# A residual turned round: tokens on the partitions, wide weights moving, gates as rows

## The reference

```python
h = rms_norm(x, gain) * (1 + scale) + shift      # shift, scale, gate come from a condition vector
y = stage(h)                                      # attention mixer, swiglu, conv/ssm mixer
x = x + gate * rms_norm(y, gain2)                 # first block (4 steps: f0, cd, f1, f2 follow them)
x = x + f * gate * y                              # second block (3 steps: in2, f3, end follow them)

def rms_norm(x, w):                               # over the 1024 features of a token
    return x * rsqrt(mean(x * x, axis=-1) + 1e-6) * w

def swiglu(h, w_in, w_out):                       # 1024 -> 2 x 2816 -> 1024, four times
    gate, up = split(h @ w_in, 2)
    return (silu(gate) * up) @ w_out
```

## Time and profile before

| what | value |
|---|---|
| median of three runs | 1353.5 us (1351.81 to 1355.49) |
| the profiled execution | 1355.59 us, its span 1353.7 us |
| TensorE, busy | 1240.0 us, 92% of the span |
| VectorE, busy | 956.0 us, 71% |
| ScalarE, busy | 598.1 us, 44% |
| GpSimd, busy | 84.1 us, 6% |
| chain that ended last | PE 79%, DVE 13%, ACT 4%, DMA 3% |

### The profile page before, as it was taken

The page is one execution under the profiler, slowest core; times in us unless marked ns, Lnnn a source line. Parts: engine busy times, 40 slices in busy tenths (PEclk is TensorE's granted clock), DMA queues, the critical chain, the costliest instruction groups (busy, mean ns, idle before and its releaser), DMA issues.

```text
span 1353.7 us, 22880 instructions
## 1 busy us (share of the span) xinstructions
PE 1240.0 (92%) x9892; PEld 1169.3 (86%) x9892; DVE 956.0 (71%) x1555; ACT 598.1 (44%) x977; POOL 84.1 (6%) x117
## 2 busy tenths in 40 slices
PE   2797979899999897889999999999999888999997
PEld 1686648899999796779999989999999887999996
DVE  5974565888885875468887768887755946655554
ACT  1533354443444445454444445444443254544442
POOL 0000000000000100019600010000000000000000
PEclk9897689999999998999999999999999998999999
DMA  9880304378895391127786644777741323455540
GB/s 379 318 330 24 164 1 187 127 305 315 315 335 210 137 397 53 63 78 266 276 303 261 265 170 169 306 298 294 275 184 64 125 93 125 145 209 212 216 153 31
DMA packets 39300, 276.78 MB, mean 204 GB/s; under 512 B 4368, under 2 KB 4896, under 8 KB 6304
## 3 DMA queue, kind: packets, MB, share of 16 engines
q1 hardware_dynamic: 37152, 269.27, 52.7%
q0 software_dynamic: 1040, 3.70, 0.8%
q10 hardware_dynamic: 1008, 2.37, 0.5%
HBM read 273.72 MB, written 1.07 MB: 203 GB/s over the span
## 4 chain that ended last, share of the span: by engine, by line
PE 79%; DVE 13%; ACT 4%; DMA 3%; issue 1%; POOL 0%; SPq 0%; DVEq 0%; ACTq 0%
PE PS L377 77%; DVE LO L1274 2%; DMA raw<-WS 2%; DVE raw L1264 2%; PE PS L561 1%; DMA SC<-scratch 1%; ACT RS L895 1%; DVE TMP L1308 1%; DVE HLo L1303 1%; ACT HH L895 1%; DVE TMP L1334 1%; ACT HI L895 1%; DVE X L1338 1%; ACT SC L895 1%; DVE RS L1289 0%
## 5 line engine op out<-in xcount | busy, mean ns | idle before, releaser
L377 PE MATMUL PS<-HH,HI 128*128 128x256 f32 x1940 | 557.1, 287 | 39.5 <-ACT HH L895 23.5
L377 PE MATMUL PS<-HLo,HI 128*128 128x256 f32 x1940 | 559.2, 288 | 1.4 <-DVE HLo L1316 0.4
L377 PE MATMUL PS<-HH,LO 128*128 128x256 f32 x1940 | 553.3, 285 | 0.0
L1274 DVE TENSOR_TENSOR LO<-raw,HI 128x1024 fp32r<-128x1024 f32 x340 | 403.7, 1226 | 123.0 <-ACT HI L895 123.0
L377 PEld LDWEIGHTS PS<-HH,HI 128*128 128x128 f32 x1940 | 376.8, 194 | 45.4 <-ACT HH L895 27.0
L895 ACT ACTIVATE HI<-raw 128x1024 fp32r<-128x1024 f32 x340 | 339.5, 1049 | 119.1 <-PE PS L377 86.6
L377 PEld LDWEIGHTS PS<-HLo,HI 128*128 128x128 f32 x1940 | 376.0, 194 | 6.6 <-DVE HLo L1303 4.0
L377 PEld LDWEIGHTS PS<-HH,LO 128*128 128x128 f32 x1940 | 377.0, 194 | 0.5 <-issue 0.5
L1264 DVE CUSTOM_DVE_ANT_0 raw<-raw,CB,SM 128x1024 f32<-128x1024 f32 x168 | 210.5, 1284 | 15.5 <-DMA raw<-WS 15.5
L377 PE MATMUL PS<-HDH,LO 128*128 128x256 f32 x716 | 202.5, 283 | 0.0
L377 PE MATMUL PS<-HDL,HI 128*128 128x256 f32 x716 | 202.1, 282 | 0.0
(11 more groups left out here) (199 smaller groups left out, 997.5 us busy)
## 6 DMA issues: line engine op xcount, KB each, us to landing
raw<-WS SPq DMA_DIRECT2D x255, 1024.0 KB, 5.3
SC<-scratch POOLq DMA_DIRECT2D x2, 1024.0 KB, 13.2
X<-xT ACTq DMA_DIRECT2D x1, 1024.0 KB, 7.1
SC<-ssm POOLq DMA_DIRECT2D x2, 512.0 KB, 4.2
out<-TMP SPq DMA_DIRECT2D x1, 1024.0 KB, 3.9
CB<-vecs SPq DMA_DIRECT2D x1, 512.0 KB, 6.3
SC<-SC ACTq DMA_DIRECT2D x4, 128.0 KB, 8.8
CB<-vecs POOLq DMA_DIRECT2D x1, 512.0 KB, 8.0
```

The source lines that it names most:

```text
L377: return e.matmul(o, l, r, start=start, stop=stop, skip_group_check=True)
L1274: e.tensor_tensor(LO[:, s % HL, :], raw_half(j, h), HI[:, s % HL, :].bitcast(fp32), O.subtract).then_inc(*D.up(("lo", s)))
```

## The change

X is kept with the tokens on the partitions: two groups of 128 tokens, 1024 features in a row. In the output projections and the down projections the activations become stationary (128 tokens) and the weights move, 512 columns at a time; the products lie in PSUM as rows (`acc_rows`, two banks for each token group). The mean of squares becomes a row sum that ACT's Square accumulates (`row_sums`, `add_normed`), one number for each token, and the root is taken of 128 x 2 values. For the next stage the features must be on the partitions again: TensorE turns X by a product with a diagonal that carries the root (`dg`), sixteen fp32 matmuls of 128 columns into banks 0 to 3, all of them ahead of the stage's first product, and DVE scales and shifts from PSUM. The gate times the gain, so far a column for each group of features (GV, 128 x 8), is needed as a row on all partitions: POOL writes GV to DRAM and reads it back as a broadcast (`gate_row`), issued at k = 2 of a projection or at j = 19 of a feed-forward block. All of `total` but two places, `new_squares` and POOL's additions go. The weights of the projections are laid out in another way on the host. The core of the diff (the first part is of TensorE; `row_sums` and the first `add_normed` are ScalarE's, the second `add_normed` and `add_gated` VectorE's, `gate_row` POOL's):

```diff
-            def linear_out(name):
-                w.wait_ge(*D.at(("hlo", name, 7)))
-                for n in range(8):
-                    key = (name, n // 2)
-                    wt = [x.rearrange("p (k n) -> p k n", k=8) for x in weight(key, n % 2)]
-                    for k in range(8):
-                        i = mm3(acc_tile(n), [x[:, k, :] for x in wt], H2[k], k, n % 2 == 0 and k == 0, k == 7, name)
-                    i.then_inc(*P.up(("acc", name, n), used(key, n % 2)))
+            def rows(name, acts, k, wt, first, last, done):
+                for qt in range(2):
+                    a = [x[:, k, qt * 128:qt * 128 + 128] for x in acts]
+                    for h in range(2):
+                        o, c = PS[:, 2 * qt + h, :], slice(h * 512, h * 512 + 512)
+                        mm(o, a[0], wt[0][:, c], first, False)
+                        mm(o, a[0], wt[1][:, c], False, False)
+                        i = mm(o, a[1], wt[0][:, c], False, last)
+                        if last and qt + h < 2:
+                            i.then_inc(*P.up(("acc", name, 2 * qt + h)))
+                i.then_inc(*P.up(("acc", name, 3), *done))
...
+            def modulate(tag, sc, fill=0):
+                mods(sc + 8)
+                busy_wide(fill)
+                for k in range(8):
+                    if k > 3:
+                        w.wait_ge(*D.at(("tmp", tag, k - 4)))
+                    for qt in range(2):
+                        w.wait_ge(*D.at(("dg", tag, qt)))
+                        i = mm(turned(k)[:, qt * 128:qt * 128 + 128], X[:, qt, k * 128:k * 128 + 128], dg[:, qt, :],
+                               k < 4 and qt == 0, True)
+                    i.then_inc(*P.up(("xt", tag, k)))
...
+            def row_sums(tag, src, ready):
+                w.wait_ge(*A.now())
+                for qt in range(2):
+                    w.wait_ge(*ready(qt))
+                    fn(junk[qt], src(qt), F.Square, accum_out=s_[:, qt:qt + 1]).then_inc(*A.up(("s", tag)))
+                w.wait_ge(*A.now())
+                w.wait_ge(*G.at("consts"))
+                first_root(tag)
...
+            def add_normed(tag, name):
+                for b in (1, 0, 3, 2):
+                    w.wait_ge(*P.at(("acc", name, b)))
+                    if b % 2 == 0:
+                        w.wait_ge(*D.at(("gy", tag, b)))
+                    fn(junk[b // 2][:, b % 2 * 512:b % 2 * 512 + 512], PS[:, b, :], F.Square, accum_out=h_[:, b:b + 1]) \
+                        .then_inc(*A.up(("sq", tag, b), ("s", tag + "y")))
+                w.wait_ge(*D.at(("v", tag + "y")))
+                first_root(tag + "y")
...
+            def add_normed(tag, name):
+                w.wait_ge(*ROWIN.at(("grow", tag)))
+                for b in range(4):
+                    w.wait_ge(*P.at(("acc", name, b)))
+                    if b % 2:
+                        w.wait_ge(*A.at(("sq", tag, b)))
+                    c = slice(b % 2 * 512, b % 2 * 512 + 512)
+                    e.tensor_tensor(gy[b // 2][:, c], PS[:, b, :], grow(tag)[:, c], O.mult).then_inc(*D.up(("gy", tag, b)))
+                w.wait_ge(*A.at(("s", tag + "y")))
+                e.tensor_tensor(s_, h_[:, 0:4:2], h_[:, 1:4:2], O.add).then_inc(*D.up(("v", tag + "y")))
+                row_root(tag + "y")
+                for qt in range(2):
+                    e.scalar_tensor_tensor(X[:, qt, :], gy[qt], r_n[:, qt:qt + 1], X[:, qt, :], O.mult, O.add) \
+                        .then_inc(*D.up(("x", tag, qt)))
...
+            def add_gated(tag, name):
+                for qt in range(2):
+                    gated_rows(tag, name, qt)
+                    w.wait_ge(*D.now())
+                    e.tensor_tensor(X[:, qt, :], X[:, qt, :], gy[qt], O.add).then_inc(*D.up(("x", tag, qt)))
...
+            def gate_row(tag):
+                n = stages.index(tag)
+                w.wait_ge(*D.at(("gv", tag)))
+                e.dma_start(bass.AP(gates_out.tensor, n * 1024, [[1, 128], [128, 8]]), GV[:, :], allow_slow_non_contiguous=True) \
+                    .then_inc(*ROWOUT.up(tag, by=16))
+                w.wait_ge(*ROWOUT.at(tag))
+                e.dma_start(grow(tag), gates_out[n:n + 1, :].to_broadcast([128, 1024])) \
+                    .then_inc(*ROWIN.up(("grow", tag), by=16))
```

More of the change, by code:

```diff
@@ L187, in mods, with build @@
         return self.catch_up(self.at_unit[last, 1], 2)
-def build(nc, xT, small, vecs, ssm, consts, firsts, WS, scratch, out):
+def build(nc, xT, small, vecs, ssm, consts, firsts, WS, scratch, gates_out, out):
     fp32 = mybir.dt.float32
@@ new lines, in linear_out @@
+            def linear_out(name, gcol, ks=range(8)):
+                if len(ks) == 8:
+                    w.wait_ge(*D.at(("hlo", name, 7)))
+                for k in ks:
+                    if k == 2:
+                        mods(gcol + 8)
+                    key = (name, k // 2)
+                    wt = weight(key, k % 2)
+                    w.wait_ge(*A.at(("hh", name, k)))
+                    w.wait_ge(*D.at(("hlo", name, k)))
+                    rows(name, (HH, HLo), k, wt, k == 0, k == 7, [used(key, k % 2)])
@@ L479, in total @@
+            def total(ps, k, tag, first, last):
+                w.wait_ge(*D.at(("total", tag, k)))
+                x = mm(ps[:, 0:256], means2[:, :], SQ[:, k, :], first, last)
                 if last:
                     x.then_inc(*P.up(("sum", tag)))
[L482 to L489, removed]
@@ L513, in down @@
                     w.wait_ge(*D.at(("hdl", tag, j)))
[L514 to L522, removed]
+                    rows(tag, (HDH, HDL), j % 3, wt, j == 0, j == 21, [("down", tag, j), used(key, j % 2)])
                 for j in range(22):
@@ L863, in pe @@
             linear_fm(("glu", 0), G2, "glu", 4, 4, [1])
[L865 to L875, removed]
+            linear_out("o2", 136, range(4))
             ps = take(("xs", "ssmy"))
             for k in (0, 2):
-                total(ps, k, 512, "ssmy", k == 0, k == 2)
+                total(ps, k, "ssmy", k == 0, k == 2)
             banks.give(("xs", "ssmy"))
[L880 to L888, removed]
+            linear_out("o2", 136, range(4, 8))
+            modulate("f3", 152, 16)
+            ffn("f3", lambda j: None, 160)
         def act(e):
@@ L1233, in act @@
             e.preload_act_table_set(LNEXP)
-            for n in range(6):
-                high(walk.weight(("o2", n // 2), n % 2))
+            linear_out("o2", 136, range(4))
             squares("ssmy", lambda j: Y[:, j, :], lambda j: D.at(("gl", j)), n=4)
@@ L1359, in ffn @@
+            def ffn(tag, later, steps, after, row):
                 for j in range(22):
@@ L1376, in ffn @@
                         .then_inc(*D.up(("hdl", tag, j)))
+                    if j == 19:
+                        gate(after, *row)
                     if j > 1:
                         use((tag, "dn", (j - 2) // 2), j % 2)
+                for _ in later:
+                    pass
                 use((tag, "dn", 10), 0)
@@ L1753, in dve @@
                     e.tensor_tensor(Y[:, j, :], Y[:, j, :], GE[:, j, :], O.mult).then_inc(*D.up(("gl", j)))
-            for n in range(6):
-                low(walk.weight(("o2", n // 2), n % 2))
+            linear_out("o2", "f3", (136, 1.0, None), range(4))
             for k in (0, 2):
```

313 lines of the change are left out of this document (142 added, 171 removed).

## The result

The changed kernel takes 1343.0 us (median of four runs, 1341.8 to 1346.6) against 1354.0 (1351.8 to 1355.5) for the kernel before beside it: ratio 0.9924, 95% interval 0.9900 to 0.9949. It is faster, by 11 us (0.8%); forecast were 30. It was the longest of the four (1346.6 us, 3.6 above their median), so the sums show some 2 us less gain than the medians.

What follows compares the result with a forecast made beforehand. TensorE, busy 92% of the span, was taken as the limit inside feed-forward blocks, with waits between them. Gains of 44.1 us, less 3 for clock and 10.7 for gate rows, gave 30.4: 1353.5 to 1323 us, range 1306 to 1346.

Steps and rivals of the forecast that it cites:

- ab: First modulation: row sums stand behind two high halves, so the first product starts later and no load hides it; -2.4 us.
- o2: Projection where all of k 0..3 now lies before the wait for k = 4, leaving 48 wide products; +5.7 us.
- w: Time for the gate vector's write to DRAM to land, in 1024 pieces of 4 bytes; taken as 8 us, bounds 5.5 to 17.6.
- (b): Rival: wide matmuls save nothing, 0.238 us each or by the page's rule; 1338 to 1340 us, chance 0.10.
- (c): Rival: TensorE's clock falls in every head, six times 3.5 instead of 3 us; 1341 us, chance 0.15.
- Gate rows: Heads waiting for the gate row's DRAM write and broadcast read-back: 0.6 us in f0, 10 in f2; -10.7 us.
- T0: End of a stage's last product; the head runs from there to the last low half of the next modulation.
- Wide matmuls: Down and output projections: 512-column products at 0.2257 us replace two of 256, saving 0.0137 each; +17.1 us, low end 2.
- It counts in full only because TensorE is the limit there: Condition on the 17.1 us from wide products: TensorE never stops inside a feed-forward block, VectorE busy 97 of 170 us.
- Normed heads: Heads of f0, cd, f1, f2: shorter chain to the last low half, gaining 6.6, 5.6, 6.4, 6.9; +25.5 us.
- Clock: Heads: 3 us without work before the turns lowers TensorE's clock in some of them; -3 us (0 to -21).
- Gated heads: Heads of in2 (-0.7) and f3 (-2.5) and the end (+1.4), with the new chain and turns; sum -1.8 us.

Runs made afterwards that it cites:

- early rows: Changed kernel with gate vectors of f0, f1, f2 and f3 computed and written to DRAM once their modulation columns exist, read-back still late: 1326.3 us, ratio 0.9787.
- early rows and fillers: Kernel with early rows, plus 34 instead of 24 filler products in the normed heads and 26 instead of 16 in in2 and f3: 1321.0 us, ratio 0.9741.

## Why the prediction missed

The direction, the range and the structure of the heads held. The size did not: 11 us for 30. In the spans 21.5 us are missing (30.4 for 8.9). The rows cost 14.1 us more than forecast. Outside them the four feed-forward stages fell short by another 10, mainly because the wide products gave little in the down projections; cd and ab fell short by 4.5. Against that, in2, o2 and the end gave 4.2 more than forecast, and the 3 us set aside for the clock are in the stages already. With w = 11, nearly what the write took, the prediction's own formulas give 1332; that 1343 still lies in the range of 1306 to 1346 is owed to the room that the range left for (b) and (c). By its own steps:

- **Gate rows, -10.7: mis-sized, and the largest error.** The runs show 24.8 us of head time, f0 5.9 for 0.6, f1 6.2 for 0, f2 11.7 for 10, f3 1.0 for 0; 18.5 us in the time of the kernel. The write landed in 10.7 us and not 8, the read-back in 9.5 and not the 8.0 of the one other broadcast. In f0 the write was issued at 216.3 instead of 211.3, since abo began at 208.4 instead of 205.1 and its first ten products ran at the lower clock (0.50 from 208.0 to 212.5 us); 10.8 us lie between write and read-back instead of 8.6, and the read-back took 10.1 instead of 8.0. The row came at 237.2 instead of 227.9, 9.3 us later, while T0 itself came 4.0 later (232.5 for 228.5), on a row that had no slack: 0.6 + 5.3 = 5.9, which is what was measured. The working's rule, a landing at T0 + R costs R + 1.25, thus held; its inputs did not. (For f2 its own inputs give w + 0.9 and not w + 2.) A wait that sits at its threshold answers in full. The rival with w of 11 to 15 and 1335 to 1350 (0.10) is nearly the case that came, with the wide products' part of (b) beside it.
- **Wide matmuls, +17.1: the step that failed most in kind.** The pitch 0.2257 came from fillers. The output projections bear it out, 0.2267 for real products with a weight load each; at this pitch the 192 of abo and cdo are worth the 2.6 us of the forecast. But 1056 of the 1248 are in the down projections, and between those it is 0.235, as PE's timeline at the end of f1 shows (18 products from the first to the last start, then the fillers):

```profile
787.78 0.39 PE L395 MATMUL PS<-HI,HDH 128*128 128x512 f32 x1
...
791.77 0.39 PE L395 MATMUL PS<-HI,HDL 128*128 128x512 f32 x1
792.00 5.61 PE L395 MATMUL PS<-HH 128*128 128x512 f32 x24
```

  (791.77 - 787.78) / 17 = 0.2347, the fillers (5.61 - 0.40) / 23 = 0.2265. For them the low end, 0.238, was the better one. The measured 0.027 per step for twelve instructions fewer is 2.3 ns each, near the 2.5 ns that the Trainium skill gives ("TensorE: Matmul & The Clock Gate", "Wait — 56ns, not 53.3ns?"); in the output projections an instruction fewer is worth 13 ns, so the traces here do not follow one such price. With the operands' new roles, which the prediction did not price, the steps give 0.086 x 88 = 7.6 us if TensorE is the limit in all. In the profile less arrives: from the last half of the head to the next T0 the four blocks gained 1.6, 1.2, -0.9 and -1.0 us, where 3.6 each was forecast. In f3 it took 4.5 us more from T0 to VectorE's product of step 4, 1.0 of it the row (2.5 were forecast for the head), and the steps behind it gave 1.5 back.
- **"It counts in full only because TensorE is the limit there": true of f3 alone.** That window was f3's. With 20 us of TensorE's work taken out of each block, the steps of f3 gave 18.5, those of f0 only 4, of f1 9, of f2 15.
- **Normed heads, +25.5: right where no row was late.** With early rows the last halves stand at 16.5, 16.7, 17.6 and 16.1 (forecast 16.1, with 1.5 more in f1). The block of f0 then takes 201.6 us from T0 to T0, 8.7 less: 6.9 in the head (6.6 were forecast) and 1.8 in what follows (3.6 were forecast). From the first turn to the first product it is 5 us and not 3.5, at a lower clock (mean 0.69 over the turns of cd in the changed kernel); at full clock 4.0.
- **cd, 3.9 for 6.9.** The head gave its 5.2. Behind it the stage lost 1.3 us instead of winning 1.3 in cdo; in 18 us of the attention (from 511 to 529) the mean granted clock was 0.66 against 0.81 before. What lowers it there was not tried. The profiles of five runs whose code differs in this stage at most in the gate rows give 137.0 to 140.4 us for it, so the missing 3 us can't be told from the spread of single executions.
- **Clock, -3.** Filling the pause in six heads was worth 5 to 6 us with the rows in time; in three heads with the rows late, 4 to 8. The turns ran at a lower clock in every head, as rival (c) has it, but that cost 6 us and not its 21: the forecast's 3 us were the nearer size.
- **Gated heads, ab, o2, end.** in2 14.4 for 14.2 and the end 11.6 for 12.2 came as forecast; ab cost 2.6 us with abo for 1.1 (T0 at 232.5 for 229.9; in six other runs with nearly the same code up to there it came at 230.2 to 234.2, a spread as large as the difference). In o2, T0 came 13.6 us after the wait for k = 4 (12.7 were forecast, 19.2 before), so that part came as forecast; in2 and o2 together gave 8.7 for 5.0, since the wait for k = 4 itself ended 3.1 us earlier, counted from the T0 of in2, where the forecast had it 0.9 later. f3 lost 2.8 instead of winning 1.1, 1.0 of it to its row.

## What to carry over

A small vector that must change from partitions to a row is cheap in bytes and dear in time: two dependent transfers, the first with 1024 pieces of 4 bytes, 20 us from issue to use beside the weights. Write it when its value exists, not when its reader is near; the vectors here existed 100 us earlier. A pitch read on one kind of product, a filler or another projection, held for one user of it and failed for the other: read it on the products that carry most of the sum. And before a saving on a full engine is counted, ask in each block whether the second engine is nearly full too, since "100% busy" in one window says nothing of the others.

## What was not expected

- TensorE in the short products of the state-space part (FB, SC) ran through in the changed kernel (in2 and o2: 124.6 us), but stopped for 1.3 to 3.0 us in the middle of them in the kernels with early rows, with no wait that the profile shows, and the granted clock over some 40 us around them was 0.91 to 0.83 instead of 1.00:

```profile
1004.80 2.28 PE L399 MATMUL PS<-FB,SC 32*128 32x63 f32 x71
1009.41 6.86 PE L399 MATMUL PS<-FB,SC 32*128 32x63 f32 x129 [2.33 <-issue]
```

  (the kernel with early rows and fillers). Before the change TensorE waited 3.9 us for VectorE in the same stage. The stop stands in all five kernels with early rows and in none of the other five changed ones. These five also have the write for f3 in that stage, and the stop ends some 17 us after its issue (16.5 to 17.2); whether one has to do with the other was not tried. So 4 to 9 us of this stage depend on something that no edit here aimed at; its cause stays open.
- With the operands' roles exchanged, the narrow products of the down projections take 0.059 us less per step of 24 (2.5 ns each), those of the output projections the same as before. The experiments do not say why.
